# First attention taken head by head, with values as the stationary operand

## The reference

```python
def attend_block(args):
    qn, qr = args
    s = (jnp.einsum('bqhd,bkhd->bhqk', qn, k_nope, preferred_element_type=jnp.float32)
         + jnp.einsum('bqhr,bkr->bhqk', qr, k_rope, preferred_element_type=jnp.float32))
    p = jax.nn.softmax(s * scale, axis=-1).astype(v.dtype)
    return jnp.einsum('bhqk,bkhd->bqhd', p, v)
```

## Time and profile before

| what | us |
|---|---|
| median of 3 runs (lowest, highest) | 4365.32 (4359.59, 4369.93) |
| the profiled execution | 4363.4 |
| its span | 4361.6 |
| PE busy, share of the span | 4020.7, 92% |
| DVE, ACT, POOL busy | 2972.8, 2432.9, 1235.0 |

### The profile page before, as it was taken

One profiled execution on the slowest core, in us unless ns is written; L12 is line 12 of the kernel. 1 busy time (PEld: TensorE's weight loads), 2 busy tenths in 40 slices (PEclk: granted clock), 3 DMA queues, 4 the chain that ended last, 5 costly groups with the idle time before them and its releaser, 6 DMA issues. The chain is left out here.

```text
span 4361.6 us, 61136 instructions
## 1 busy us (share of the span) xinstructions
PE 4020.7 (92%) x21445; PEld 3411.2 (78%) x21445; DVE 2972.8 (68%) x3831; ACT 2432.9 (56%) x3867; POOL 1235.0 (28%) x846
## 2 busy tenths in 40 slices
PE   8989799999997998999799999997698799999995
PEld 8978688888776876888578888886687588888782
DVE  6667555555487885444477777774655799999885
ACT  7634333333313554333388888887422577777773
POOL 0000145445310110000288888884000111111114
PEclk9999899999998998999899999998899899999998
DMA  6667733333496433222440000004543688888987
GB/s 230 220 211 244 234 101 114 105 112 120 145 280 194 142 106 119 67 68 74 105 157 15 15 23 15 15 10 153 192 155 111 230 317 318 319 323 330 370 332 290
DMA packets 417337, 728.63 MB, mean 167 GB/s; under 512 B 121744, under 2 KB 314384, under 8 KB 396304
## 3 DMA queue, kind: packets, MB, share of 16 engines
q1 hardware_dynamic: 382560, 642.02, 42.9%
q10 hardware_dynamic: 20640, 50.87, 3.3%
q0 software_dynamic: 13968, 33.58, 2.1%
HBM read 601.84 MB, written 213.91 MB: 187 GB/s over the span
## 5 line engine op out<-in xcount | busy, mean ns | idle before, releaser
L2675 POOL TENSOR_TENSOR a_PL<-a_PT,a_PH 128x512 fp32r<-128x512 f32 x512 | 673.7, 1331 | 133.8 <-ACT a_PH L2794 129.8
L2844 DVE TENSOR_REDUCE a_part<-a_pA 128x1 f32<-128x1024 f32 (+1 forms) x384 | 359.8, 954 | 96.1 <-PE a_pA L2698 91.6
L2792 ACT ACTIVATE a_PT<-a_pB 128x512 f32<-128x512 f32 x576 | 340.5, 591 | 79.1 <-PE a_pB L2721 77.6
L2794 ACT ACTIVATE a_PH<-a_PT 128x512 fp32r<-128x512 f32 x576 | 364.2, 632 | 18.4
L3478 POOL DMA_INDIRECT w_XG<-between_h,all_slots x65 | 123.4, 1899 | 783.3 <-PE e_pT L3761 720.9
L1397 ACT ACTIVATE a_PT<-a_pT 128x512 f32<-128x512 f32 x128 | 69.6, 595 | 409.0 <-PE a_pT L1327 408.9
L1432 DVE TENSOR_REDUCE a_maxima<-a_pS 128x1 f32<-128x512 f32 x256 | 176.0, 688 | 131.1 <-PE a_pS L1309 129.8
L1341 PE MATMUL a_pO<-a_V,a_PT 128*128 128x128 f32 x2048 | 250.4, 275 | 1.0 <-DVE a_PT L1445 1.0
L1341 PEld LDWEIGHTS a_pO<-a_V,a_PT 128*128 128x128 f32 x2048 | 244.3, 192 | 6.5 <-DVE a_PT L1445 1.2
L1239 POOL TENSOR_TENSOR a_QL<-a_RQ,a_QT 128x512 fp32r<-128x512 f32 x16 | 20.6, 1285 | 797.8 <-DVE a_QP L1467 797.8
L2739 PE MATMUL a_pO<-a_PL,a_VH 128*128 128x512 f32 x576 | 225.6, 392 | 3.1 <-DVE a_PL L2854 2.0
(11 more groups left out here) (651 smaller groups left out, 10611.0 us busy)
## 6 DMA issues: line engine op xcount, KB each, us to landing
w_gate<-in_moe_w_gate SPq DMA_DIRECT2D x47, 2048.0 KB, 7.8
w_up<-in_moe_w_up SPq DMA_DIRECT2D x47, 2048.0 KB, 12.4
w_down<-in_moe_w_down SPq DMA_DIRECT2D x46, 2048.0 KB
between_yb<-e_Y ACTq DMA_DIRECT2D x46, 512.0 KB, 7.1
a_row_w<-in_w_ada SPq DMA_DIRECT2D x16, 1024.0 KB, 5.4
between_x<-m_X SPq DMA_DIRECT2D x32, 512.0 KB, 2.8
between_yb<-a_zeros SPq DMA_DIRECT2D x32, 512.0 KB, 14.2
between_tv<-pz_OV SPq DMA_DIRECT2D x16, 576.0 KB, 2.9
```

The lines of the kernel that those rows point to most:

```text
L2675: pool.tensor_tensor(PL[:, t % RING, :], PT[:, t % RING, :], PH[:, t % RING, :].bitcast(F32), ALU.subtract).then_inc(S["p_low"], 1)
L2792: act.activation(PT[:, t % RING, :], pB[t % 2][:], ACT.Exp, scale=scale).then_inc(S["p_ready"], 1)
L2794: act.activation(PH[:, t % RING, :], PT[:, t % RING, :], ACT.Copy).then_inc(S["p_high"], 1)
L2844: dve.tensor_reduce(part[:, h, r % (NG2 // G4):r % (NG2 // G4) + 1], src, AX_X, ALU.max).then_inc(S["maxed"], 1)
```

## The change

The stage is written for the one attention that uses it. Units run head by head, and two query tiles of a head form a pair; 32 pairs, 64 slots. A slot u has the scores of unit u, the turning of unit u-1, and half the products of an earlier pair: the values of a head are split into high and low parts as well (`VH`, `VL`), a key tile of them is the stationary operand, and the turned probabilities of both query tiles, high and rest side by side (`PT`), move through: one matmul of 512 columns, one of 256. ACT copies each turned group out as the high part, DVE subtracts it from the bank to get the rest. The result comes with the value's index on the partitions; ACT and DVE add its halves (`OT`), PE turns it back in two transposes, DVE divides. The three small jobs hang on every fourth slot ("quarter" i has slots 4i to 4i+3). Keys and values of heads 0 and 1 load at the start, those of heads 2 and 3 a head ahead. Loops are unrolled.

```diff
+            def pair(q):
+                if q + 2 < PAIRS:
+                    wait(S["q_split"], q + 2)
+                    load_query(q + 2)
+                if q >= 3:
+                    store(q - 3)
...
+            def quarter(i):
+                load_row(i)
+                h = i // 4
+                if i % 4 == 1 and 1 <= h < H1 - 1:
+                    wait(S["p_ready"], GROUPS * NT * h)
+                    load_keys(h + 1)
+                    wait(S["o_ps"], PER_HEAD * h)
+                    load_values(h + 1)
+                pair(2 * i)
+                if i:
+                    store_split(i - 1)
+                load_split(i)
...
+                pair(2 * i + 1)
+                if i:
+                    store_row(i - 1)
...
+            def bank_free(what, u):
+                if turned[what, u] >= 2:
+                    pe.wait_ge(S["moved"], turned[what, u] - 1)
...
-                for j in range(groups[g][1]):
-                    jj = 4 * g + j
-                    mm = pe.matmul(pO[:, 0:dv], PT[:, jj, :], values(V, h, jj), start=jj == 0, stop=jj == key_tiles - 1)
+                def rests(j):
+                    return pe.matmul(pO[:, 0:PW], VL[h % 2][:, j, :], PT[:, j, 0, :], start=False, stop=False)
+
+                for j in range(4 * g, 4 * g + 4):
+                    if j:
+                        rests(j)
+                    mm = pe.matmul(pO[:], VH[h % 2][:, j, :], PT[:, j].rearrange("p a b -> p (a b)"), start=j == 0, stop=j == NT - 1)
...
+            def slot(u):
+                q, second = u // 2, u % 2
+                here, turns, applies = u < UNITS, 1 <= u <= UNITS, 2 <= u < UNITS + 2
+                for g in range(GROUPS):
+                    if here:
+                        scores(u, g)
+                    if turns and g < 2:
+                        turn(u - 1, g)
+                    if g == 2 and u >= 4:
+                        back(u - 4)
+                    if g >= 2 and second and applies:
+                        apply(q - 1, g)
+                    if g == 3 and turns:
+                        turn(u - 1, 2)
+                        turn(u - 1, 3)
+                if not second and applies:
+                    apply(q - 1, 0)
+                    apply(q - 1, 1)
...
+            def move(u, g):
+                high = PT[:, 4 * g:4 * g + 4, 0, queries(u)]
+                dve.wait_ge(S["high_moved"], u * GROUPS + g + 1)
+                dve.tensor_tensor(PT[:, 4 * g:4 * g + 4, 1, queries(u)], bank_of(g, u)[:].rearrange("p (a b) -> p a b", b=P), high.bitcast(F32),
+                                  ALU.subtract).then_inc(S["moved"], 1)
...
+                if u % 2 == 0 and u + 2 < UNITS:
+                    high_queries(u // 2 + 1)
+                if u % 4 == 1:
+                    split(i)
+                if u % 4 == 3 and i:
+                    modulation(i - 1)
+                if u % 4 == 0 and i >= 2:
+                    row(i - 2)
```

More of the change, by code:

```diff
@@ L1059, with attention_1 @@
 ROW = 256
-def attention(nc, I, C, D, M, stage, copied, heads, dv, key_tiles, scale, nope, key_sets, sets_of_head, value_parts, parts_of_head, load_query,
-              query_dmas, values, out):
+def attention_1(nc, I, C, D, M):
     with ExitStack() as ctx:
[L1077 to L1092, removed]
@@ L1117, in attention, with bank_of, highs_ready, queries @@
         S = {n: k.sem(n) for n in names}
[L1118 to L1122, removed]
-        block = ctx.enter_context(nc.Block())
[L1125 to L1144, removed]
+        k_loaded, v_loaded, row_loaded, stored = ([k.sem(f"{n}{b}") for b in range(2)] for n in ("k_loaded", "v_loaded", "row_loaded", "stored"))
+        block = ctx.enter_context(nc.Block())
+        turned = {}
+        for u in range(1, UNITS + 4):
+            for what in (0, 1, "back", 2, 3):
+                if what == "back":
+                    if u >= 4:
+                        turned["back", u - 4] = len(turned)
+                elif u <= UNITS:
+                    turned[what, u - 1] = len(turned)
+        def bank_of(what, u):
+            return pT[turned[what, u] % 2]
+        def highs_ready(h):
+            return 1 + 2 * h
+        def queries(u):
+            return slice((u % 2) * P, (u % 2 + 1) * P)
         @block.sync
@@ L1192, in tile @@
[L1192 to L1208, removed]
@@ L1218, in load_scan @@
                 load_inputs(sp, D, M["inputs_0"], 0, M["inputs_loaded"])
[L1220 to L1226, removed]
+            load_query(0)
+            sp.dma_start(KRL[:].bitcast(F32), D["kr"]).then_inc(S["kr_loaded"], 16)
+            load_keys(0)
@@ L1287, in _ @@
[L1287 to L1289 removed]
+            low_queries(0)
+            pool.wait_ge(S["kr_high"], 1)
+            pool.tensor_tensor(KRL[:, pool_keys], KRL[:, pool_keys].bitcast(F32), KRH[:, pool_keys].bitcast(F32), ALU.subtract).then_inc(S["k_split"], 1)
+            low_values(0)
+            k.clear_spent(pool)
+            for i in range(QUARTERS):
+                h = i // 4 + 1
+                low_queries(2 * i + 1)
+                if i % 4 == 3 and h < H1:
+                    low_values(h)
+                modulation(i)
+                if i + 1 < QUARTERS:
+                    low_queries(2 * i + 2)
+                row(i)
+                if i % 4 == 2 and h < H1:
+                    low_keys(h)
@@ L1365, in modulation @@
                 mm.then_inc(S["ada_ps"], 1)
-            def row(t):
-                pe.wait_ge(S["row_summed"], t.i + 1)
-                pe.wait_ge(S["row_added"], t.i + 1)
-                pe.wait_ge(S["ada_moved"], t.i + 1)
-                pe.matmul(pC[:, ROW:2 * ROW], C["ones"][:], row_w[t.b][:, 0, :], start=True, stop=True).then_inc(S["row_ps"], 1)
-            def tile(t):
-                for h in range(heads):
-                    for g in range(banks):
-                        scores(t, h, g)
-                        if not (t.first and h == 0):
-                            of_unit_before(between[g], t, h)
-                    if h == 1 and not t.first:
-                        modulation(t.before())
-                if not t.first:
-                    row(t.before())
@@ L1384, in _, with row @@
-            tiles(pe, NT, tile)
-            modulation(tile_at(NT - 1))
-            for steps in between:
-                of_unit_before(steps, tile_at(NT), 0)
-            row(tile_at(NT - 1))
+            def row(i):
+                pe.wait_ge(S["row_summed"], i + 1)
+                pe.wait_ge(S["ada_moved"], i + 1)
+                pe.matmul(pC[:, ROW:2 * ROW], C["ones"][:], row_w[i % 2][:, 0, :], start=True, stop=True).then_inc(S["row_ps"], 1)
+            def slot(u):
[16 more added lines that the diff above has]
+                    apply(q - 1, 1)
@@ L1390, in _ @@
+            for u in range(UNITS):
+                slot(u)
+                if u >= 4 and u % 4 == 1:
+                    modulation(u // 4 - 1)
+                if u >= 4 and u % 4 == 3:
+                    row(u // 4 - 1)
+            modulation(QUARTERS - 1)
+            for u in range(UNITS, UNITS + 4):
+                slot(u)
+            row(QUARTERS - 1)
         @block.scalar
         def _(act):
-            def move(t, h):
-                u = unit(t, h)
-                for g in act_moves:
-                    m = groups[g][1]
-                    act.wait_ge(S["t_ps"], u * banks + g + 1)
-                    act.activation(PT[:, 4 * g:4 * g + m, :].rearrange("p a b -> p (a b)"), pT[g % 2][:, 0:m * P], ACT.Copy).then_inc(S["act_moved"], 1)
@@ L1422, in _ @@
+            high_keys(0, 0, 1)
+            high_values(0, 0, 1)
             act.wait_ge(S["c_loaded"], 48)
             act.activation(half_c[:], cc[:], ACT.Tanh, scale=0.5).then_inc(S["tanh_done"], 1)
-            tiles(act, NT, tile)
-            move(tile_at(NT - 1), heads - 1)
+            for u in range(UNITS + 3):
+                slot(u)
+                h = u // NT + 1
+                if h < H1 and u % NT in (8, 9):
+                    high_keys(h, u % NT - 8, 2)
+                if h < H1 and u % NT in (10, 11):
+                    high_values(h, u % NT - 10, 2)
@@ L1532, in _ @@
-            finish(tile_at(NT - 1), heads - 1, 1)
-            modulation(tile_at(NT - 1))
-            row(tile_at(NT - 1))
+            for u in range(UNITS):
+                slot(u)
+                i = u // 4
+                if u % 2 == 0 and u + 2 < UNITS:
[6 more added lines that the diff above has]
+                    row(i - 2)
@@ L1535, in _ @@
+            row(QUARTERS - 2)
+            modulation(QUARTERS - 1)
+            for u in range(UNITS, UNITS + 4):
+                slot(u)
+            row(QUARTERS - 1)
             dve.wait_ge(S["ada_moved"], PIECES)
```

505 lines of the change are left out of this document (261 added, 244 removed).

## The result

The kernel after takes 4510.4 us (median of four runs, 4506.0 to 4512.1) where the one before took 4364.4 in the same session: a ratio of 1.0323 (95% interval 1.0306 to 1.0340), 146 us slower. The prediction had the side and the place right, and half the size: 4435 was forecast, with a range that ended at 4488.

What follows compares the result with a forecast made beforehand. PE alone bounded the stage. First quarter 38, fifteen of 44.1 + 0.8, less 3.6, plus 12 and 0.5: 720.4 against 650.3, +70, so 4435 us; forecast's own range 4405 to 4470, overall 4368 to 4488.

Steps and rivals of the forecast that it cites:

- Products, PE's list: Products take matmuls of 0.23 and 0.12 us; PE's own list falls from 20.1 to 19.0 us a pair.
- rival B: PE stays the bound by its list alone, 38.0 + 0.7 us a quarter: -34, 4331 us; chance 0.09.
- Moves: DVE's subtraction for a turned bank, after ACT's copy, costs 0.68 us; neither engine fills up.
- Waits 1 and 2: Odd slots: late exponentials idle PE 1.15 us, twice a quarter; gate row matmul waits for DVE's modulation copy, +0.9.
- L: Start of a slot's last score matmul, from which the prediction counts times in us.
- Wait 3: DVE's split waits 3.1 us for reloaded w_out_2 columns, reaching PE whole; the loop makes a quarter 44.1 against 40.87.
- the clock: PE's clock lowered after a wait of about 3 us: 0.8 us a quarter, bounds 0 and 1.7.
- the keys: Key and value loads ahead of the split stores in two quarters: 12 us in all, bounds 0 and 21.
- the split's price: DVE's split of the reloaded w_out_2 columns, up to the next maximum: 1.1 us.
- the reload: Gate row's end to reloaded tile landed: 12.8 us, including 0.5 for the 1 MB load before the split stores.
- The ends: Stage's start and end: first keys load a little earlier, two slots of drain added, +0.5 us.
- Rival C: SP's queue fills, reload lands 16 us after the row, clock lost each time: 49.0 a quarter, 4497 us; chance 0.12.

Runs made afterwards that it cites:

- experiment 10: Changed kernel with split two slots later, third turn before the last four key tiles, POOL's low_keys and SP's load_scan later: 4340.2 us, ratio 0.9948 to the kernel before.
- Experiments 4: Changed kernel with POOL's modulation cut to two groups of weights, halving sums left out: 4511.4 us; stage 756.9 against 789.0 us.
- experiment 5: On top of experiment 2, POOL's modulation moved behind its split of the next queries: 4407.6 us, ratio 1.0091 to the kernel before.
- experiment 2: Changed kernel with the split columns' stores and the reload first in SP's quarter: 4471.5 us, ratio 1.0252 to the kernel before.
- experiment 3: Changed kernel with 40 extra matmuls before PE's second turn in the slot behind the split: 4486.4 us, ratio 1.0286 to the kernel before.
- experiment 9: Changed kernel with only the third turn moved ahead of the last four key tiles in odd slots: 4483.7 us, ratio 1.0284 to the kernel before.

## Why the prediction was wrong in its size

- **Products, PE's list: right.** The pair's matmuls take 0.23 and 0.12; rival B's 38.7 a quarter, PE's list alone, is nearly what experiment 10 reaches. The gain was there.
- **Moves: right.** The subtraction takes 0.68, as the copy in the earlier trace rows.
- **Waits 1 and 2: right.** Next scores at L + 3.68 (864.55 to 868.23) for 3.6, and at L + 4.38 with the row (892.87 to 897.25) for 4.5. Removing the cause of wait 1 gave 0.8 to 1.4 a slot.
- **Wait 3: the mechanism right, its loop mis-sized.** Term by term in the quarter shown (us):

| term | forecast | measured |
|---|---|---|
| row's end to reload landed | 12.8 | 13.46 (859.10 to 872.57) |
| split to the next maximum | 1.1 | 2.99 |
| maximum to the next slot's scores | 8.2 + 0.8 for the clock | 10.48 (875.56 to 886.04) |
| odd slot with the row | 11.3 | 11.21 |
| even slot | 9.7 | 9.92 |
| to the next row's end | 1.0 | 1.41 |
| quarter | 44.9 | 49.5 (mean of the ordinary twelve 49.1) |

Fifteen quarters of 4.2 are 63 of the 68.6 us that the stage came out above the forecast; the scan's tables add 9, and the keys took 8.9 instead of 12.

The step that failed first is the split's price. I took 1.1 from the earlier trace rows, where it stands behind the gate row and POOL has finished, and carried it to a place where POOL computes; there it took 2.99, and 3.2 on average over the twelve. Experiments 4 and 5 show that POOL is the cause: with POOL done early the split is fast though its columns have just landed (4), and with SP's order of experiment 2 kept it falls from 5.9 to 1.1 when POOL's modulation alone is moved (5). DVE's gate row, at the end of the loop, took 0.84 beside POOL's split of the queries, where the earlier trace rows has 0.43; that this has the same reason is read from the rows, no run takes POOL away there. The Trainium skill, "SBUF — State Buffer" (SBUF: two separate sides), says that DVE and GpSimd share one pair of SBUF ports, which a GpSimd operation or a DVE operation in a two-port mode or with two inputs in SBUF, whichever starts first, holds for its whole instruction; in which mode this cast runs no run here shows. Otherwise the runs agree: a slowed cast or subtraction of the columns ends 0.3 to 0.6 us behind one of POOL's instructions (859.65 behind 859.37, 793.83 behind 793.28), and DVE's maximum of a PSUM bank keeps its 0.68 beside POOL (875.56).

The second is the clock. I took 0.8, half of what the row with 3.33 us of idle time lost, since the one with 3.12 lost nothing and I expected a wait like these. The wait was 5.75, and experiment 3 gives 1.7, the upper bound; at full clock the 8.2 came out as 8.4 there. So the rule of the Trainium skill's page "TensorE: Matmul & The Clock Gate" (HAM oscillation) that the prediction weighed holds for this loop, with the wait as long as it became: the granted clock is 0.50 to 0.65 in the four microseconds behind each of the fifteen waits.

The third is the reload: the second split store, behind the row's load, took 5.6 to land (3.4 in experiment 2, where it stands ahead of that load), so the chain gained 1.2 (13.46 - 12.3) where I had put 0.5, between 0 and 2.3.

The scan's tables I overlooked. Before, SP issued them behind the last reload; the change puts them ahead of the last quarter's chain, where DVE waits 11.9 us for the reload: 26.2 for that slot. The ends, +0.5 forecast, took 4.1 (the drain 4.8 more, the start 0.7 earlier).

Rival C came nearest in number (4497), but not by what it says: the reload lands 13.5 behind the row, not 16, and 1.9 us of the quarter shown are the slow split's, which no rival had.

Two workings of the prediction don't come out as written, and neither bore on the result. The 42.9 a quarter at the low end of the range lies 2.0 under 44.9, while the terms named for it, 0.5, 0.8 and 0.1, make 1.4. The 3 us per MB of the keys is right, but it is 5.3 - 3.0 for the 0.75 MB between the two loads of the earlier trace rows, not 5.3 - 2.3.

## What to carry to other kernels

A job that is moved has to be priced against what the other engines do at the new place, not by the row of the old place; here it was POOL beside DVE's operations from SBUF to SBUF. Look for the loop that a reused buffer closes (store, landing, reload, next use) and count its length against the slots that it now has; shortening a slot beside the chain gave nothing (experiment 9). Then move the job out of the loop's way: two slots were worth 120 us.

## What was not expected of the hardware

- Beside POOL's tensor operations, DVE's cast of 128x512 from SBUF to SBUF took up to 3.6 us instead of 0.42, and its subtraction up to 4.95 instead of 0.69; POOL's multiplication lost nothing by it (3.63 against 3.62), its sums up to 0.3.
- Behind loads of 2 MB of keys and values SP's next issue stood for 6.5 us (experiment 5) to 7.7 (the kernel after).
